# Expert blocks of a hybrid S5/HGRN2 step: two halves of 32 tokens per weight chunk, with expert weights loaded in pairs

## The reference

```
scores = sigmoid(x @ router_w)                  # 16 experts in 4 groups
expert = the two best of the best group         # per token
y      = (silu(x @ w_gate[e]) * (x @ w_up[e])) @ w_down[e]
out    = sum over a token's two experts of weight * y
```

## Time and profile before

| | us |
|---|---|
| median of 3 runs | 1439.46 |
| lowest and highest | 1433.66, 1447.06 |
| profiled execution, its time | 1438.59 |
| profiled execution, its span | 1436.8 |
| PE busy in the span | 1337.9 (93%) |
| mean granted TensorE clock | 0.969 |

### The profile page before, as it was taken

How to read it: one execution, slowest core, us unless ns; L and a number is a source line. 1 busy time by engine, 2 the same in 40 slices (tenths; PEclk the granted TensorE clock), 3 DMA queues, 4 the chain that set the end, 5 groups by cost and what they waited for, 6 DMA issues and landing times.

```text
span 1436.8 us, 25808 instructions
## 1 busy us (share of the span) xinstructions
PE 1337.9 (93%) x10155; PEld 837.8 (58%) x10156; DVE 414.1 (29%) x886; ACT 263.3 (18%) x401; POOL 235.1 (16%) x285
## 2 busy tenths in 40 slices
PE   5899999977999999999958999999999999999975
PEld 3688778756676677764434455555555555454532
DVE  4692870375622210113362000000000000000065
ACT  3305002243125000001111111111111111111102
POOL 0033403200000000000023022012022222223310
PEclk9899999998999999999979999999999999999997
DMA  7459632345430412514088619819949999999993
GB/s 303 150 130 391 149 71 68 80 148 194 148 131 3 177 44 78 215 39 167 15 336 343 257 44 383 340 29 350 393 151 398 379 403 381 404 379 397 383 401 122
DMA packets 92365, 322.30 MB, mean 224 GB/s; under 512 B 12000, under 2 KB 12384, under 8 KB 91536
## 3 DMA queue, kind: packets, MB, share of 16 engines
q1 hardware_dynamic: 72304, 268.77, 49.5%
q0 software_dynamic: 11216, 38.41, 8.7%
q10 hardware_dynamic: 8784, 14.24, 3.2%
HBM read 286.18 MB, written 33.10 MB: 222 GB/s over the span
## 4 chain that ended last, share of the span: by engine, by line
PE 72%; DMA 13%; DVE 5%; issue 3%; SPq 3%; ACT 2%; POOL 0%; POOLq 0%; DVEq 0%; ACTq 0%
PE ps L2236 18%; PE ps L1771 11%; PE ps L2247 10%; PE ps L1759 9%; DMA expert_w<-in_w_down 9%; PE ps L2150 5%; PE ps L2199 5%; SPq L557 3%; PE ps L1863 2%; PE ps L1946 2%; DMA expert_w<-in_w_up 2%; PE ps L2242 1%; DMA x_sorted<-h,router_ints 1%; PE ps L1832 1%; PE ps L2226 1%
## 5 line engine op out<-in xcount | busy, mean ns | idle before, releaser
L2236 PE MATMUL ps<-expert_w,x_block_t 128*64 128x256 f32 x3584 | 403.8, 382 | 15.1 <-issue 6.5
L2236 PEld LDWEIGHTS ps<-expert_w,x_block_t 128*64 128x64 f32 x3584 | 256.0, 137 | 163.1 <-issue 31.5
L2247 PE MATMUL ps<-expert_w,act_t 128*64 128x512 f32 x896 | 213.9, 604 | 3.6 <-DMA expert_w<-in_w_down 2.6
L1771 PE MATMUL ps<-h_t,weight_ring 128*128 128x320 f32 x640 | 178.4, 435 | 0.0
L1771 PEld LDWEIGHTS ps<-h_t,weight_ring 128*128 128x128 f32 x640 | 121.5, 191 | 50.9 <-issue 2.8
L1759 PE MATMUL ps<-h_t,weight_ring 128*128 128x320 f32 x512 | 145.4, 447 | 2.8 <-ACT h_t L749 2.8
L1669 DVE TENSOR_TENSOR activations<-silu_tmp,ps 128x256 f32<-128x256 f32 x56 | 23.6, 421 | 375.9 <-ACT silu_tmp L967 375.9
L1759 PEld LDWEIGHTS ps<-h_t,weight_ring 128*128 128x128 f32 x512 | 100.1, 197 | 45.2 <-issue 6.9
L2247 PEld LDWEIGHTS ps<-expert_w,act_t 128*64 128x64 f32 x896 | 57.8, 136 | 103.1 <-issue 78.2
L692 POOL COPY expert_w<-staged 128x1024 f32<-128x1024 f32 x42 | 43.9, 1044 | 414.5 <-PE ps L2236 269.0
L1690 DVE COPY y_block<-ps 128x512 f32<-128x512 f32 x25 | 17.3, 692 | 188.7 <-PE ps L2247 188.7
(11 more groups left out here) (362 smaller groups left out, 1224.2 us busy)
## 6 DMA issues: line engine op xcount, KB each, us to landing
expert_w<-in_w_down SPq DMA_DIRECT2D x128, 512.0 KB, 13.2
weight_ring<-in_stream SPq DMA_DIRECT2D x98, 512.0 KB, 4.9
expert_w<-in_w_gate SPq DMA_DIRECT2D x58, 512.0 KB, 11.8
expert_w<-in_w_up SPq DMA_DIRECT2D x58, 512.0 KB, 12.8
staged<-in_w_gate SPq DMA_DIRECT2D x28, 512.0 KB, 14.0
gathered<-in_w_gate SPq DMA_DIRECT2D x28, 512.0 KB, 16.0
gathered<-in_w_up SPq DMA_DIRECT2D x28, 512.0 KB, 16.5
x_sorted<-zero POOLq DMA_DIRECT2D x18, 512.0 KB, 13.8
```

The source lines that it names most:

```text
L1771: last = mm(pair(job)[:, a, :], w[:, k, :], h_t[:, k, a * HALF:(a + 1) * HALF], start=(k == 0), stop=(k == KD - 1))
L2236: last = mm(ps[MB * g:MB * g + MB, 2 * half + w, 0:256], x_blk_t[:, 2 * kp + k2, :], rows[:, at_col:at_col + 256], start=(kp == 0 and k2 = ...
L2247: last = mm(ps[MB * half:MB * half + MB, 4, :], act_t[:, 4 * (f // 4) + 2 * (f % 2) + f // 2 % 2, :], w_slot[3 * f + 2][:, 4 * half:4 * ha ...
```

## The change

Each block is worked in two halves of 32 tokens (`h`). The stationary operand is 32 tokens wide and four products stand side by side in four column groups (`Q = 4`). A gate-and-up step `gates(h, k)` has four products of 512 moving columns (gate and up in one tile), and each weight chunk is used for both halves before the next, except the last two chunks, where half 0 is finished first. `down(h, j)` has four products of 256 moving columns. The last two blocks use `down_both` (64 tokens wide, 512 columns). The order of K and of the hidden features is such that a quarter of the features stands on 32 partitions, so that DVE can turn both the tokens and the product with its 32 x 32 transpose (`turn_x`, `turn_act`); the transposes on PE and the copies on ACT go. The slots become 12 tiles of 1 MB (8 KB on each partition): 8 of gate and up (`w_gu`), 4 of two down chunks (`w_dn`); what was loaded with two DMAs is loaded with one. Staged loads stay at 512 KB. Tokens are loaded and stored by halves, with a DRAM side of 4 x 32 rows of 256 features. PE's loop ends two blocks earlier, like those of ACT and DVE, and the last two blocks are written out.

```diff
-        w_slot = [at(f"expert_w{s}", end - s * 4096, [P, KD, P]) for s in range(3 * KF)]
-        x_blk = at("x_block", qs0, [P, 512])
+        w_gu_sb = [at(f"expert_gu{k}", end + 4096 - (u + 1) * 8192, [P, 2, D]) for k, u in enumerate(GU_PLACE)]
+        w_dn_sb = [at(f"expert_dn{m}", end + 4096 - (u + 1) * 8192, [P, 2, D]) for m, u in enumerate(DN_PLACE)]
+        x_blk = at("x_block", qs0, [P, 2, QC])
...
-                    sp.dma_start(w_slot[3 * f][:, :, :], w_gate[bass.ds(e, 1), f, :, :, :]
-                                 .rearrange("a p k c -> p (a k) c")).then_inc(gu_in[f], 16)
-                    sp.dma_start(w_slot[3 * f + 1][:, :, :], w_up[bass.ds(e, 1), f, :, :, :]
-                                 .rearrange("a p k c -> p (a k) c")).then_inc(gu_in[f], 16)
+                    sp.dma_start(w_gu_sb[f][:, :, :].rearrange("p w c -> p (w c)"), w_gu[bass.ds(e, 1), f, :, :, :]
+                                 .rearrange("a p w c -> p (a w c)")).then_inc(gu_in[f], 16)
...
-                for f in range(KF):
-
-                    sp.wait_ge(down_done, b * KF + (f + 1))
-                    sp.dma_start(w_slot[3 * f + 2][:, :, :], w_down[bass.ds(e, 1), f, :, :, :]
-                                 .rearrange("a p k c -> p (a k) c")).then_inc(dn_in[f], 16)
+                for m in range(DN):
+                    sp.wait_ge(down_done, b * KF + (2 * m + 2))
+                    sp.dma_start(w_dn_sb[m][:, :, :].rearrange("p j c -> p (j c)"), w_dn[bass.ds(e, 1), m, :, :, :]
+                                 .rearrange("a p j c -> p (a j c)")).then_inc(dn_in[m], 16)
...
             def load_x(row):
-                for g in range(2):
-                    act.dma_start(x_blk[MB * g:MB * g + MB, :], x_sorted[bass.ds(row, MB), 512 * g:512 * g + 512])\
+                for h in range(2):
+                    act.dma_start(x_blk[:, h, :], x_sorted[bass.ds(row + SUB * h, SUB), :].rearrange("t (q c) -> q t c", q=Q))\
                         .then_inc(x_blk_in, 16)
...
-                    for half in range(2):
-                        act.dma_start(y_sorted[bass.ds(i * MB, MB), 512 * half:512 * half + 512],
-                                      y_blk[MB * half:MB * half + MB, :]).then_inc(y_stored, 16)
+                    for h in range(2):
+                        act.dma_start(y_sorted[bass.ds(i * MB + SUB * h, SUB), :].rearrange("t (q c) -> q t c", q=Q),
+                                      y_blk[:, h, :]).then_inc(y_stored, 16)
...
+            def turn_act(h):
+                vec.transpose(act_t[:, :, h, :], acts[:, h, :].rearrange("p (j l) -> p j l", l=SUB)).then_inc(act_ready, 1)
+
+            def turn_x():
+                vec.transpose(x_blk_t[:, :, :, :].rearrange("p h k t -> p (h k t)"),
+                              x_blk[:, :, :].rearrange("p h c -> p (h c)")).then_inc(xt_copied, 1)
...
+            def gates(h, k):
+                for g in range(Q):
+                    last = mm(ps[SUB * g:SUB * g + SUB, h, :].rearrange("p (w c) -> p w c", w=2), x_blk_t[:, h, k, :],
+                              w_gu_sb[k][:, :, QC * g:QC * g + QC], start=(k == 0), stop=(k == KD - 1))
+                if h == 1:
+                    last.then_inc(gu_done, 1)
+                elif k == KD - 1:
+                    last.then_inc(half_done, 1)
...
+            def down(h, j):
+                for g in range(Q):
+                    last = mm(ps[SUB * g:SUB * g + SUB, 4 + h, 0:QC], act_t[:, j, h, :],
+                              w_dn_sb[j // 2][:, j % 2, QC * g:QC * g + QC],
+                              start=(j == 0), stop=(j == KF - 1))
...
-            blocks = pe.value_load(rint[0:1, TOTAL:TOTAL + 1], min_val=EXPERTS, max_val=NBLK)
+            last2 = pe.value_load(rint[0:1, LAST2:LAST2 + 1], min_val=EXPERTS - 2, max_val=NBLK - 2)
```

More of the change, by code:

```diff
@@ L2240, in turn_act @@
-            def turn_act(a):
-                for j in range(2):
-                    last = nc.tensor.transpose(ps[:, 5 + 2 * a, j * P:(j + 1) * P], acts[:, a, j * P:(j + 1) * P], ident)
-                last.then_inc(act_turned, 1)
-            def down(f):
+            def gates(h, k):
[6 more added lines that the diff above has]
+                    last.then_inc(half_done, 1)
@@ new lines, in _ @@
+            both = KD - 2
+            tail_gates = [(0, k) for k in range(both, KD)] + [(1, k) for k in range(both, KD)]
+            tail_downs = [(h, j) for j in range(KF // 2, KF) for h in range(2)]
+            def down(h, j):
[3 more added lines that the diff above has]
+                              start=(j == 0), stop=(j == KF - 1))
+                if h == 1:
+                    last.then_inc(down_done, 1)
@@ L2280, in _ @@
-            pe.wait_ge(route_ready, 1)
-            blocks = pe.value_load(rint[0:1, TOTAL:TOTAL + 1], min_val=EXPERTS, max_val=NBLK)
+            for k in range(both):
+                pe.wait_ge(gu_in[k], 16)
+                gates(0, k)
+                gates(1, k)
+            for h, k in tail_gates:
+                if h == 0:
+                    pe.wait_ge(gu_in[k], 16)
+                gates(h, k)
+            for h in range(2):
+                pe.wait_ge(act_ready, h + 1)
+                for j in range(KF // 2):
+                    if h == 0 and j % 2 == 0:
+                        pe.wait_ge(dn_in[j // 2], 16)
+                    down(h, j)
@@ L2309, in _ @@
-                pe.nop()
-            pe.wait_ge(pick_ready, 1)
-            pe.wait_ge(xt_copied, blocks + 1)
-            pe.nop()
-            for n in range(2 * CH):
-                last = nc.tensor.transpose(ps[:, (7, 5, 6)[n // 4], (n % 4) * P:(n % 4 + 1) * P],
-                                           pick[:, n // CH, n % CH, :, :].rearrange("p a t -> p (a t)"), ident)
-            last.then_inc(pick_turned, 1)
+                    for k in range(both):
+                        wait_gates(e, k)
+                        gates(0, k)
+                        gates(1, k)
@@ new lines, in _ @@
+                    for j in range(KF // 2):
+                        down(1, j)
+                    for h, j in tail_downs:
+                        if h == 0 and j % 2 == 0:
+                            pe.wait_ge(dn_in[j // 2], e * 16 + 16)
+                        down(h, j)
+                pe.nop()
+            for u in range(2):
+                e = pe.value_load(rint[0:1, bass.ds(last2 + u, 1)], min_val=0, max_val=EXPERTS - 1)
+                pe.wait_ge(xt_copied, last2 + (u + 1))
+                for k in range(both):
+                    wait_gates(e, k)
+                    gates(0, k)
+                    gates(1, k)
+                for h, k in tail_gates:
+                    if h == 0:
+                        wait_gates(e, k)
+                    gates(h, k)
+                pe.wait_ge(y_copied, last2 + (u + 1))
+                if u == 0:
+                    pe.wait_ge(pick_ready, 1)
+                    for n in range(2 * CH):
+                        last = nc.tensor.transpose(ps[:, (7, 5, 6)[n // 4], (n % 4) * P:(n % 4 + 1) * P],
+                                                   pick[:, n // CH, n % CH, :, :].rearrange("p a t -> p (a t)"), ident)
+                    last.then_inc(pick_turned, 1)
+                pe.wait_ge(act_ready, last2 * 2 + (2 * u + 2))
+                for j in range(KF):
+                    if j % 2 == 0:
+                        pe.wait_ge(dn_in[j // 2], e * 16 + 16)
+                    down_both(j)
```

273 lines of the change are left out of this document (121 added, 152 removed).

## The result

The changed kernel takes 1520.1 us (median of 4 runs, 1516.6 to 1524.3) against 1440.8 us before (median of 4 beside them): ratio 1.055, 95% interval 1.050 to 1.061. It is slower by 5.5%; the forecast was 1503 us. The profiled execution has a span of 1519.2 us against 1436.8.

A forecast was written before the change was run, and what follows sets the result against it. PE-bound blocks alternate with DMA-bound stretches. Cycles +39.5, three stretches +31.8, first stretch +6, last stretch +3.7, PE-bound blocks -9.5, end -7.5: together +64.0 on 1438.6 us, predicted 1503 us; own range 1488 to 1532, with milder cases and room 1440 to 1550.

The forecast's parts named there:

- Four engines: Token transfers: a DRAM side beginning with 4 runs on four engines, 1.17 us more per transfer, 86 us; forecast's chance 0.70.
- eight engines: Rival on token transfers: eight engines share each, 0.39 us more per transfer, 1446 us; chance 0.04.
- no concentration: Rival on token transfers: they stay spread over 16 engines, the 86 us go, 1417 us; chance 0.14.
- one direction: Rival on token transfers: only loads or only stores gather on four engines, 43 of 86 us go, 1460 us; chance 0.10.
- column groups: Rival on PE: four column groups overlap only two at a time with longer products, 2013 us; chance 0.02.
- PE-bound block: Five blocks inside long experts: 20.5 us in place of 22.46, 1.9 us saved each, together -9.5 us.
- The price of a packet: Token transfers: a 1 KB packet costs an engine 0.049 us, half a 2 KB packet's price; bounds 0.0425 and 0.0975.
- By stretch: DMA-bound stretches, from a long expert's last block to the next one's first: three at +10.6 us, the first +6.
- three cycles: Three DMA-bound cycles of three blocks, 81.7 us each in place of 68.5: +13.2 us each, together +39.5.
- the last stretch and the end: Last two experts' loads +3.7 us; end -7.5, from 10.6 saved less 3 uncovered (bounds -2 and -10.6).
- Weight packets: 1 MB weight loads with 8 KB packets: gain bounded at 3%, taken as 1.5%, 0.020 us per slot.
- The chain: In the cycles the chain of waits still runs over down loads, and PE waits 15 to 20 us per cycle.

The follow-up runs named there:

- two-engine run: Against the changed kernel, tokens moved with a DRAM side of 2 x 32 x 1 KB, four loads and four stores per block; 1684.8 us.
- tokens spread: Against the changed kernel, token loads and stores each in four transfers with 32 partitions first, so on 16 engines; 1424.5 us, ratio to before 0.990.
- halves at 512 KB loads: The changed kernel with tokens on 16 engines and all weights in 512 KB loads of 4 KB packets; 1438.3 us, ratio to before 0.999.
- the run with 4 KB packets: The changed kernel, tokens still on four engines, all weights in 512 KB loads; 1526.8 us, ratio to before 1.058.

## Why the prediction was right, and where it was off

*Four engines.* Right, and for the reason given, the count that the DRAM side begins with: four small packets per transfer, the drop to a quarter of the rate, and 96 us back when it begins with 32. The two-engine run shows the same rule at another count, as the Trainium skill has it (DMA: Bandwidth & Descriptors, "Why a DMA increments its semaphore by 16 and not by 1"); which engines they are, no row shows. The rivals of eight engines and of no concentration are out, that of one direction too: both directions cost. That of column groups is out with the PE-bound block of 20.95 us.

*The price of a packet.* 0.049 us taken, 49 ns measured. Half of a 2 KB packet's price was a choice between bounds of 0.0425 and 0.0975, so that it hit is in part luck.

*The two parts.* The forecast is 86 us for the four engines less 22 us for the rest. Measured are 96 and 15.

*By stretch.* The forecast's sum against the two profiles, from SP's starts (before: 772.32, 858.65, 972.61, 1063.49, 1337.51 us, and the span's end, 1436.8; after: 773.54, 862.29, 983.13, 1080.76, 1409.05, and 1519.2):

| | forecast | measured |
|---|---|---|
| up to the first DMA-bound expert's end, with two PE-bound blocks | +2.2 | +3.6 |
| second stretch, two PE-bound blocks | +6.8 | +6.9 |
| third, one | +8.7 | +6.7 |
| fourth, and three cycles | +50.2 | +54.3 |
| last stretch and end | -3.8 | +10.9 |

(The forecast's terms regrouped: +10.6 per stretch, +13.2 per cycle, -1.9 per PE-bound block, +6 for the first stretch.) Up to the last stretch the sum is right within 4 us. The PE-bound block saved 1.5 us, not 1.9. Part of this agreement is luck. With tokens spread a cycle takes 67.5 us, where the forecast's terms give 67.9; but the packets gain 2.0 us per cycle and not 0.57, and against them stand 1.8 us by which a cycle is longer with halves at 512 KB loads (70.3 us against 68.5), which the forecast hasn't and for which no run shows the cause.

*The step that failed* is the last stretch and the end, +3.7 and -7.5, off by 14.7 us of the 18.4 by which the sum misses the difference of the two profiles. Two things stand in its place. First, with tokens spread this stretch takes 98.5 us and with four engines 110.2: 11.7 us, where four transfers of 1.17 more are 4.7. Here landing time does count: the gathers wait for the last store, which lands after 25.8 us and not 9.8,

```profile
1420.84 25.82 DMA y_sorted<-y_block
```

so POOL's first gather (1447.61) comes 38.6 us behind SP's last start, where with spread tokens (1348.17) it is 23.3. Second, without the four engines the forecast's terms save 8.5 us here, and the run with spread tokens saved 0.8 (99.3 to 98.5). The end itself came as forecast: from the last down product to DVE's first sum it is 3.0 us in place of 13.4 (1403.90 to 1406.88; on four engines 1499.71 to 1502.69):

```profile
1489.83 9.88 PE ps L2256 x32
...
1502.69 1.24 DVE final L1725
```

But the last down product ends 79.0 us behind SP's last start and not 69.4, so 9.6 us of delay were uncovered where I had estimated 3. The chain of gathers and additions, not the last down loads, now ends last there. With 512 KB loads the stretch is 94.5 us, so the 1 MB loads cost 4.0 us where I had 0.6.

*Weight packets.* I bounded the gain at 3% from one row of 32 KB packets. The packets gained 5% (1376 to 1303 ns per slot). That bound was too tight. With tokens on four engines the 1 MB loads were worth 6.7 us in all (1526.8 to 1520.1).

*The chain.* I expected PE's waits over down loads; they came over the store. In the cycles this made little difference: a second buffer took the store off the chain and left the time, smaller packets took away 7 us at most. The store's late landing and the down load's lag are the same four full engines seen from two queues.

## What to carry to other kernels

Before a tile is cut in another shape, look at what the outermost count of each of its transfers becomes: here 4% of the kernel's bytes (13.7 of 322 MB), put on 4 of 16 engines, cost 96 us of 1520, since every weight load is spread over all 16 and has landed only when the fullest engine has done its part. The sign of it is a rate that falls to a fraction while loads are still awaited. When a chain of waits ends in one transfer's landing, ask what the engines under it are doing before adding a buffer: here the buffer moved the row and not the time. And where PE and the loads are within 2% of each other, two edits that each gain nothing can gain together, so they have to be tried as a table of four.

## What the runs showed of the hardware that was not expected

- A block's store, 64 packets on an engine and 3 us by itself, took 28 to 33 us to land beside a queue of 8 KB packets (0.34 us each): as if one packet of each queue went in turn, 64 x (0.34 + 0.05) = 25 us. That is argued from the numbers, and the 25 fall short of the 28 to 33; the run with 4 KB packets fits it in its shorter waits.
- Issuing itself took time. ACT's instruction that starts a store takes 0.61 us in the changed kernel at the median, and up to 8.9; with two engines the one that starts a load takes up to 15.0, and four of them from 1291.66 us on are 30 us of the chain in a cycle of 102.4. ACT takes no silu meanwhile. The cycle was still the sum of the engines' work, so I count this as another sight of full engines; no run parts the two.
- Some of the down products ran at a lower clock in the DMA-bound stretches. The 128 products at 1224.77 us took 9.27 us at a mean granted clock of 0.76, those at 1389.25 8.95 at 0.79, those at 942.53 8.74 at 0.81; at 1.00 they take 6.95. PE had stood idle for 10.83, 10.86 and 2.50 us right before them. All three stand on the chain, 6 us together, which the forecast hadn't.
- Cycles of about 75 and 89 us took turns with four engines and 1 MB loads, with one result buffer and with two, but not with 512 KB loads (80 to 83 each), at the same mean of 82.1. Why is open.
- With the tokens spread and 512 KB loads a cycle is 70.3 us, 1.8 more than in the kernel before, with the same bytes. At the start of a cycle the DMA share is low (0.5 and 0.8 in the first two slices of 1.8 us); no run was made on the cause.
